# Samples' attention one pair of heads later, the last key pages in two parts, and the output projection's first unit split ahead of the samples' outputs

## The chip, the core and the metric

The kernel runs on one core of one Trainium2 chip. The metric is the device time of one execution in microseconds (us), and lower is better. The engines are named as in the profile: PE is TensorE's matmuls, PEld its weight loads, DVE is VectorE, ACT is ScalarE, POOL is GpSimd, SP is SyncE (here it only issues DMAs, as SPq). PE's clock is granted at one of two levels, 1.2 GHz (0.50 in the profile's column PEclk) and 2.4 GHz (1.00).

## What is computed

One inference step of a two-layer decoder, all in float32, for a prompt of 256 tokens and for 8 samples with one new token each and 256 cached keys in two pages. Layer 0 is gated linear attention and a dense SwiGLU; then a shared key/value projection; layer 1 is stick-breaking attention and a top-2-of-8 mixture of experts. The part that matters here is layer 1's mixer, for both groups of tokens:

```python
def stick_breaking_attention(q, k, v, bias, q_offset):
    ...
        z = jnp.einsum('bqhd,bkhd->bhqk', qb, kb) * (SB_HEAD_DIM ** -0.5) + bias_f
        ...
        log1m = jnp.where(mask, jax.nn.log_sigmoid(-z), 0.0)
        later = lax.cumsum(log1m, axis=3, reverse=True) - log1m
        log_att = jnp.where(mask, log1m + z + later, -jnp.inf)
        outs.append(jnp.einsum('bhqk,bkhd->bqhd', jnp.exp(log_att), vb))

def sb_mixer(h, k_all, v_all, q_offset, w_q, b_sb, w_out):
    ...
    o = stick_breaking_attention(q, k_all, v_all, b_sb, q_offset)
    return o.reshape(B, L, D_MODEL) @ w_out
```

Beside it the conditioning vectors go through the modulation weights (`silu(c) @ ada_w`), of which six weight tiles are multiplied inside this stage.

## The kernel before

**The stage.** Eight pairs of heads of the prompt are worked through by one loop over `g` that every engine runs in its own hand-written order, g = 0 to 8. In step g PE does the sums over later keys of pair g (`later_sums`, L1096 and L1099), the values of pair g - 1 (`values`, L1111), perhaps one modulation tile (`ada`, L763), and the scores of pair g + 2 (`z_products`, L1080 to L1087). ACT turns scores into soft terms (`soft`, L1705 to L1707), takes the exponent (L1720) and rounds pair g - 1 to its high part (L1723). DVE finishes the soft term of pair g + 1 (`softplus`, L2235) and makes the low part of pair g - 1 (L2261).

**The samples' attention** is threaded through the same loop. DVE multiplies each sample's query with its two key pages and reduces by head (page 0: L2213 and L2215, page 1: L2219 and L2221), four pages in `scores_after(1)`, step 0. Then come the bias and an absolute value on DVE (L2267, L2269), an exponent and a logarithm on ACT (L1728, L1729), L2272 on DVE (it posts `l_s`), three small matmuls on PE (L1166 to L1168), L2275 on DVE and L1732 on ACT. From then on PE can multiply the value pages: `values_s(i)` (L1126) for i = 0 to 3, two samples each, in the steps that `OWN_DURING` gives; DVE picks the heads' own parts (`own_values`, L2251) and PE brings them into rows (`own_rows`, L1136). Once the last is there, ACT rounds the samples' rows (L1736), DVE takes the rest (L2280, it posts `os_lo`), and PE starts the output projection `sb_out`.

**The output projection** takes its weights in units: ACT copies a unit's high part (`w_hi`, L1463) and DVE makes its low part (`w_lo`, L1863), and PE needs both for L845 to L847. Its first three units wait for the end of the loop (`first_splits`).

**The weight ring.** Three buffers of 2 MB, `ring0` to `ring2`, are filled by SP strictly in the order of the list `STREAM`; before each load SP waits until the tile that lies in that buffer was used. In this stage the tiles are called here by their kind and number: a22 to a27 (modulation, `ada`), v0 to v3 (value pages), k0 to k3 (key pages), o0 and o1 (`sb_out`), a28 to a31 (the final norm's modulation, `in_final_ada_w`). The order of the loads is

```python
+ [("ada", 22)] + [t for i in range(4) for t in (("ada", 23 + i), ("v_cache", i))] + [("ada", 27)]
+ [("sb_out", i) for i in range(2)] + [("ada", i) for i in range(28, 32)])
```

that is a22, a23, v0, a24, v1, a25, v2, a26, v3, a27, o0, o1, a28. With three buffers in turn, v0 goes where k3 was, a24 where a22 was, v1 where a23 was, a25 where v0 was, and so on. A load of v0 waits until both pages of the last two samples were reduced (`z_s_ready`), one of a25 until `values_s(0)` was done (`opv_done`).

The tables that set in which step PE multiplies them are

```python
PAGES_AFTER = (((1, 4), (1, 5)), ((0, 6), (0, 7), (1, 6), (1, 7)))
ADA_DURING = {1: 22, 2: 23, 3: 24, 4: 25, 6: 26, 7: 27}
OWN_DURING = {2: 0, 3: 1, 5: 2, 6: 3}
```

Of the kernel before, what the change touches and what calls it, by code (L numbers as in the profile page):

```python
# [112 lines left out]
UNIT_AT = {t: 4 * n for n, t in enumerate(SPLIT)}  # L113
# [11 lines left out]
ELSEWHERE = 1000.0  # L125
Q_ROWS = 3
PAGES_DURING = {4: (0, 0), 5: (0, 1), 6: (1, 0), 7: (1, 1), 9: (0, 2), 10: (0, 3), 11: (1, 2), 12: (1, 3), 14: (0, 4), 15: (0, 5)}
PAGES_AFTER = (((1, 4), (1, 5)), ((0, 6), (0, 7), (1, 6), (1, 7)))
ADA_DURING = {1: 22, 2: 23, 3: 24, 4: 25, 6: 26, 7: 27}
OWN_DURING = {2: 0, 3: 1, 5: 2, 6: 3}  # L130
TURNS = [(t, q) for q in range(4) for t in range(TT)]
TURN_AFTER = {5: 0, 6: 1, 7: 2, 9: 3, 10: 4, 11: 5, 13: 6, 14: 7, 15: 8}

# [6 lines left out]
def build(nc, A, O, cap=CAP):  # L140
# [3 lines left out]
    with ctx:  # L144
# [584 lines left out]
        def _(eng):  # L729
# [419 lines left out]
            for g in range(G + 1):  # L1149
                if g < G:  # L1150
                    later_sums(g)
                if g in OWN_DURING and OWN_DURING[g] >= 1:
                    own_rows(OWN_DURING[g] - 1, g - 1)
                if g == 0:
                    eng.wait_ge(S["kv_kept"], 12)
                    eng.wait_ge(S["qs_kept"], 1)
                if g >= 1:
                    values(g - 1)
                if g in ADA_DURING:
                    ada(4 * ADA_DURING[g], 4 * ADA_DURING[g] + 4, ends=g == G - 1)  # L1160
                if g + 2 < G:
                    z_products(g + 2)
                if g == 1:
                    eng.wait_ge(S["l_s"], 1)
                    neg = pb[5][:, 0:P].rearrange("p (b h) -> p b h", b=NB), pb[5][:, P:2 * P].rearrange("p (b h) -> p b h", b=NB)
                    eng.matmul(neg[0], neg_after[:], ls[:, 0, :, :], start=True, stop=False, skip_group_check=True)  # L1166
                    eng.matmul(neg[0], neg_ones[:], ls[:, 1, :, :], start=False, stop=True, skip_group_check=True)
                    eng.matmul(neg[1], neg_after[:], ls[:, 1, :, :], start=True, stop=True, skip_group_check=True).then_inc(S["rcs_done"], 1)  # L1168
                if g in OWN_DURING:
                    values_s(OWN_DURING[g])  # L1170
# [271 lines left out]
        def _(eng):  # L1442
# [41 lines left out]
            def first_splits(kind, first=0):  # L1484
                for m in range(first, AHEAD):
                    split(UNIT_AT[kind, 0] + m, late=True)
# [213 lines left out]
            def soft(g):  # L1700
                eng.wait_ge(S["z_done"], g + 1)
                if g >= 2:
                    eng.wait_ge(S["rc_done"], g - 1)
                lg = l_buf[:, g % 2, :, :]
                link(eng.activation(lg, z_banks(g), ACT.Abs))  # L1705
                link(eng.activation(lg, lg, ACT.Exp, scale=-1.0))
                eng.activation(lg, lg, ACT.Ln, bias=1.0).then_inc(S["soft_ready"], 1)  # L1707
# [7 lines left out]
            for g in range(G + 1):  # L1715
                if g < G:
                    eng.wait_ge(S["rc_done"], g + 1)
                    if g >= 2:
                        eng.wait_ge(S["pv_done"], g - 1)
                    eng.activation(p_buf[:, g % 2, :, :], z_banks(g), ACT.Exp).then_inc(S["p_exp"], 1)  # L1720
                if g >= 1:
                    eng.wait_ge(S["pv_done"], g)
                    eng.copy(hh[:, g - 1, 0:TP], pb[4][:, 0:TP]).then_inc(S["hh_ready"], 1)  # L1723
                if g in ADA_DURING:
                    ada(4 * ADA_DURING[g], 4 * ADA_DURING[g] + 4, ends=g == G - 1)
                if g == 1:
                    eng.wait_ge(S["abs_s"], 1)
                    link(eng.activation(ls, ls, ACT.Exp, scale=-1.0))  # L1728
                    eng.activation(ls, ls, ACT.Ln, bias=1.0).then_inc(S["soft_s"], 1)  # L1729
                if g == 2:  # L1730
                    eng.wait_ge(S["args_s"], 1)
                    eng.activation(zs[:, :, :, 0:SH], zs[:, :, :, 0:SH], ACT.Exp).then_inc(S["exps_s"], 1)  # L1732
                if g + 2 < G:
                    soft(g + 2)
            eng.wait_ge(S["os_done_all"], NB // 2)
            eng.copy(hh[:, :, TP:T], rows_s).then_inc(S["os_hi"], 1)  # L1736
            first_splits("sb_out")
            split_during("sb_out", 2)

            norm(FFN1, splits=False, after=(S["kept_dve"], empt[-1][1]), during=(112, 120))  # L1740
# [104 lines left out]
        def _(eng):  # L1845
# [20 lines left out]
            def first_splits(kind, first=0):  # L1866
                for m in range(first, AHEAD):
                    split(UNIT_AT[kind, 0] + m, late=True)
# [370 lines left out]
            def scores_after(part):  # L2239
                for page, b in PAGES_AFTER[part]:  # L2240
                    (page1_scores if page else page0_scores)(b)
# [12 lines left out]
            for g in range(G + 1):  # L2254
                if g + 1 < G:
                    softplus(g + 1)
                if g == 0:
                    scores_after(1)
                if g >= 1:
                    eng.wait_ge(S["hh_ready"], IN_SB_OUT * KC + g)  # L2260
                    eng.tensor_tensor(hl[:, g - 1, 0:TP], pb[4][:, 0:TP],  # L2261
                                      hh[:, g - 1, 0:TP], ALU.subtract).then_inc(S["hl_ready"], 1)
                if g in ADA_DURING:
                    ada(4 * ADA_DURING[g], 4 * ADA_DURING[g] + 4, ends=g == G - 1)
                if g == 0:
                    eng.wait_ge(S["z_s_ready"], NB)
                    link(eng.tensor_tensor(as_rows(z_of_s), as_rows(z_of_s), sb_bias[:].unsqueeze(1).to_broadcast([P, PAGES * NB, SH]),  # L2267
                                           ALU.add))
                    eng.scalar_tensor_tensor(as_rows(ls), as_rows(z_of_s), -1.0, as_rows(z_of_s), ALU.mult, ALU.max).then_inc(S["abs_s"], 1)  # L2269
                if g == 1:  # L2270
                    eng.wait_ge(S["soft_s"], 1)
                    eng.scalar_tensor_tensor(as_rows(ls), as_rows(z_of_s), 0.0, as_rows(ls), ALU.max, ALU.add).then_inc(S["l_s"], 1)  # L2272
                if g == 2:
                    eng.wait_ge(S["rcs_done"], 1)
                    eng.tensor_tensor(as_rows(z_of_s), as_rows(z_of_s), pb[5][:, 0:256].rearrange("p (r h) -> p r h", h=SH),  # L2275
                                      ALU.add).then_inc(S["args_s"], 1)
                if g in OWN_DURING:
                    own_values(OWN_DURING[g])
            eng.wait_ge(S["os_hi"], 1)
            eng.tensor_tensor(hl[:, :, TP:T], rows_s, hh[:, :, TP:T], ALU.subtract).then_inc(S["os_lo"], 1)  # L2280
            first_splits("sb_out")
            for i in range(8):
                add_block("sb_out", i, GATE[MIX1])

# [240 lines left out]
```

## Time and profile before

| | us |
|---|---|
| median of 3 runs | 1565.06 |
| lowest, highest | 1559.33, 1565.71 |
| the profiled execution | 1560.55 |
| its span, first to last instruction | 1558.7 |
| PE busy in the span | 1499.7 (96%) |
| DVE busy | 440.3 (28%) |
| ACT busy | 325.9 (21%) |

The stage that the change touches runs from about 509 to 586 us of the span. The timeline has one line for each run of like instructions: start, duration, engine, line, what it writes and reads, how many, and in brackets how long the engine sat idle before it and what ended that. A table of stretches has for each stretch its length, each engine's busy time with its number of instructions, PE's granted clock, the mean busy share of the 16 DMA engines and the GB/s that they moved. PE's matmuls overlap, so the distance from one start to the next says more than a duration.

### The profile page before, as it was taken

The numbers are of one execution on the slowest core, as the hardware profiler recorded it, in microseconds if no ns is written. First come the engines' busy times: TensorE is split into PE (matmuls) and PEld (weight loads), VectorE is DVE, ScalarE is ACT, GpSimd is POOL, SyncE is SP. The second block draws the span as 40 slices with busy tenths as digits, with TensorE's granted clock in tenths as the row PEclk, the third lists the DMA queues.
The fourth block names the chain that finished last, engine by engine and source line by source line (L and its number), as shares of the span: only waits on it lengthen the run. The fifth ranks groups of instructions, "written<-read, shape, count | busy, mean of one in ns | idle before, by whom it ended". The sixth has DMA issues, their size and how long they took to land.

```text
span 1558.7 us, 35713 instructions
## 1 busy us (share of the span) xinstructions
PE 1499.7 (96%) x16405; PEld 894.4 (57%) x16405; DVE 440.3 (28%) x697; ACT 325.9 (21%) x505; POOL 60.1 (4%) x111
## 2 busy tenths in 40 slices
PE   6999899999999899899999999999999999999996
PEld 3995688899899557434435435335345344354353
DVE  3653663455477625210010010010020100100312
ACT  3653353444364544200000000000000000000001
POOL 2001100000000000000000000000000000001000
PEclk9999999999999899899999999999999999999996
DMA  9657878884476995999999999999999999999980
GB/s 341 234 200 268 306 267 276 311 295 172 166 264 260 372 396 217 407 365 412 405 403 424 409 405 422 410 409 410 417 411 406 415 416 406 405 425 407 409 372 30
DMA packets 118518, 535.54 MB, mean 344 GB/s; under 512 B 6347, under 2 KB 29001, under 8 KB 88674
## 3 DMA queue, kind: packets, MB, share of 16 engines
q1 hardware_dynamic: 109842, 504.42, 82.3%
q0 software_dynamic: 7584, 25.57, 4.6%
q10 hardware_dynamic: 944, 3.26, 0.6%
q8 instruction: 131, 2.15, 0.6%
q14 instruction: 17, 0.14, 0.0%
HBM read 521.38 MB, written 11.84 MB: 342 GB/s over the span
## 4 chain that ended last, share of the span: by engine, by line
PE 73%; issue 16%; DVE 4%; DMA 3%; ACT 1%; POOL 1%; SPq 0%; POOLq 0%; DVEq 0%; ACTq 0%
PE psum L1256 37%; PE psum L1268 18%; PE psum L845 3%; PE psum L846 3%; PE psum L847 3%; PE psum L763 2%; PE psum L810 1%; PE psum L961 1%; DMA ring<-in_ada_w 1%; DMA xe_rows<-h_rows,row_from 1%; DVE w_lo L1863 1%; PE psum L1269 1%; DMA ring<-in_cache_k 0%; PE psum L929 0%; DMA h<-q_scratch 0%
## 5 line engine op out<-in xcount | busy, mean ns | idle before, releaser
L1256 PE MATMUL psum<-e_ring,xe 128*32 128x512 f32 (+1 forms) x3456 | 336.1, 547 | 0.9 <-DVE xe L2372 0.9
L845 PE MATMUL psum<-hh,w_hi 128*128 128x264 f32 x864 | 250.5, 290 | 9.1 <-DVE hl L1992 2.6
L1256 PE MATMUL psum<-ring,xe 128*32 128x384 f32 (+1 forms) x2688 | 251.9, 531 | 0.0
L846 PE MATMUL psum<-hl,w_hi 128*128 128x264 f32 x864 | 246.6, 285 | 0.0
L847 PE MATMUL psum<-hh,w_lo 128*128 128x264 f32 x864 | 246.4, 285 | 0.0
L1256 PEld LDWEIGHTS psum<-e_ring,xe 128*32 128x32 f32 x3456 | 113.2, 110 | 217.7 <-issue 216.5
L1863 DVE TENSOR_TENSOR w_lo<-ring,w_hi 128x1024 fp32r<-128x1024 f32 (+1 forms) x132 | 157.7, 1206 | 141.2 <-ACT w_hi L1463 141.1
L2415 DVE TENSOR_TENSOR act_e<-silu_e,psum 128x1536 f32<-128x1536 f32 (+1 forms) x16 | 24.9, 1554 | 583.3 <-PE psum L1256 583.3
L1268 PE MATMUL psum<-ring,at 128*32 128x256 f32 x2448 | 180.4, 379 | 0.0
L1269 PE MATMUL psum<-ring,at 128*32 128x256 f32 x816 | 180.0, 379 | 0.0
L1256 PEld LDWEIGHTS psum<-ring,xe 128*32 128x32 f32 x2688 | 87.8, 110 | 159.7 <-issue 159.7
L845 PEld LDWEIGHTS psum<-hh,w_hi 128*128 128x128 f32 x864 | 164.6, 190 | 20.5 <-issue 12.4
L846 PEld LDWEIGHTS psum<-hl,w_hi 128*128 128x128 f32 x864 | 164.8, 191 | 0.0
L847 PEld LDWEIGHTS psum<-hh,w_lo 128*128 128x128 f32 x864 | 163.9, 190 | 0.0
L1463 ACT CAST w_hi<-ring 128x1024 fp32r<-128x1024 f32 (+1 forms) x132 | 135.8, 1034 | 106.3 <-PE psum L847 67.0
L1268 PEld LDWEIGHTS psum<-ring,at 128*32 128x32 f32 x2448 | 100.5, 110 | 71.0 <-issue 3.1
L1268 PE MATMUL psum<-e_ring,at 128*32 128x256 f32 x1584 | 115.6, 379 | 0.0
L1269 PE MATMUL psum<-e_ring,at 128*32 128x256 f32 x528 | 115.5, 379 | 0.0
L1789 ACT ACTIVATE silu_e<-psum 128x1536 f32<-128x1536 f32 (+1 forms) x16 | 20.6, 1290 | 439.4 <-PE psum L1256 439.4
L1268 PEld LDWEIGHTS psum<-e_ring,at 128*32 128x32 f32 x1584 | 65.6, 110 | 44.8
L1269 PEld LDWEIGHTS psum<-ring,at 128*32 128x32 f32 x816 | 89.2, 110 | 0.0
L1770 ACT COPY xe<-psum 128x384 f32<-128x384 f32 x8 | 3.8, 478 | 309.6 <-PE psum L1247 309.6
(401 smaller groups left out, 1235.4 us busy)
## 6 DMA issues: line engine op xcount, KB each, us to landing
e_ring<-in_moe_w_gate_up SPq DMA_DIRECT2D x40, 2048.0 KB, 13.3
ring<-in_moe_w_gate_up SPq DMA_DIRECT2D x24, 2048.0 KB, 15.4
e_ring<-in_moe_w_gate_up SPq DMA_DIRECT2D x32, 1536.0 KB, 13.0
ring<-in_moe_w_gate_up SPq DMA_DIRECT2D x32, 1536.0 KB, 12.4
ring<-in_ada_w SPq DMA_DIRECT2D x20, 2048.0 KB, 11.0
ring<-in_moe_w_down SPq DMA_DIRECT2D x24, 1536.0 KB, 12.6
ring<-in_moe_w_down SPq DMA_DIRECT2D x16, 2048.0 KB, 9.9
e_ring<-in_moe_w_down SPq DMA_DIRECT2D x16, 2048.0 KB
```

What stands on the lines that cost most here:

```text
L763: last = eng.matmul(part_bank(i)[g * STRIP:(g + 1) * STRIP, :], c_pad[:, k, :], cols8(slot("ada", i))[:, at, :], start=half == 0 and i == ...
L810: last = eng.matmul(pb[7][:, 0:T], ones[:], squares[:, k, :], start=k == 0, stop=k == KC - 1)
L845: eng.matmul(to, wh, ah, start=start, stop=False)
L846: eng.matmul(to, wh, al, start=False, stop=False)
L847: return eng.matmul(to, wl, ah, start=False, stop=stop)
L1256: last = eng.matmul(outs[r][s * STRIP:(s + 1) * STRIP, :].rearrange("p (c i) -> p c i", c=4), tokens[:, r * STRIP:(r + 1) * STRIP], pieces ...
L1268: eng.matmul(outs[r][strip, :], tokens[:, strip], w, start=start, stop=stop, skip_group_check=True)
L1269: last = eng.matmul(outs[r][CAP:P, :], tokens[:, r * STRIP:(r + 1) * STRIP], rest, start=start, stop=stop, skip_group_check=True)
L1463: eng.copy(unit(w_hi, kind, m, ks), quarter(slot(kind, i), kind, m % 4, ks)).then_inc(S["hi_ready"], 1)
L1789: eng.activation(silu_e[:, 0:ROUNDS * width].rearrange("p (r c) -> p r c", r=ROUNDS), psum[:, 0:ROUNDS * 512].rearrange("p (r c) -> p r c" ...
L1863: eng.tensor_tensor(unit(w_lo, kind, m, ks), quarter(slot(kind, i), kind, m % 4, ks), unit(w_hi, kind, m, ks), ALU.subtract).then_inc(S["l ...
L2415: eng.tensor_tensor(by_round(act_e), by_round(silu_e), psum[:, 3 * 512:6 * 512].rearrange("p (r c) -> p r c", r=ROUNDS)[:, :, 0:width], AL ...
```

## The change

The samples' chain, from the bias to the exponent, moves one step of g later on all three engines, and `values_s` moves to steps 3, 4, 5 and 6. The page 1 products of the last two samples (4 of the 8 instructions of `scores_after(1)`) move from step 0 to step 1 of DVE. a25 moves from step 4 to step 5. ACT and DVE split `sb_out`'s first unit before they wait for the samples' rows. What SP issues, and its order, stay as they are.

```diff
-PAGES_AFTER = (((1, 4), (1, 5)), ((0, 6), (0, 7), (1, 6), (1, 7)))
-ADA_DURING = {1: 22, 2: 23, 3: 24, 4: 25, 6: 26, 7: 27}
-OWN_DURING = {2: 0, 3: 1, 5: 2, 6: 3}
+PAGES_AFTER = (((1, 4), (1, 5)), ((0, 6), (0, 7)), ((1, 6), (1, 7)))
+ADA_DURING = {1: 22, 2: 23, 3: 24, 5: 25, 6: 26, 7: 27}
+OWN_DURING = {3: 0, 4: 1, 5: 2, 6: 3}
...
-                if g == 1:
+                if g == 2:
                     eng.wait_ge(S["l_s"], 1)
...
-                if g == 1:
+                if g == 2:
                     eng.wait_ge(S["abs_s"], 1)
...
-                if g == 2:
+                if g == 3:
                     eng.wait_ge(S["args_s"], 1)
...
+            split(UNIT_AT["sb_out", 0], late=True)
             eng.wait_ge(S["os_done_all"], NB // 2)
             eng.copy(hh[:, :, TP:T], rows_s).then_inc(S["os_hi"], 1)
-            first_splits("sb_out")
+            first_splits("sb_out", 1)
...
-                if g == 0:
+                if g == 1:
+                    scores_after(2)
                     eng.wait_ge(S["z_s_ready"], NB)
...
-                if g == 1:
+                if g == 2:
                     eng.wait_ge(S["soft_s"], 1)
...
-                if g == 2:
+                if g == 3:
                     eng.wait_ge(S["rcs_done"], 1)
...
+            split(UNIT_AT["sb_out", 0], late=True)
             eng.wait_ge(S["os_hi"], 1)
             eng.tensor_tensor(hl[:, :, TP:T], rows_s, hh[:, :, TP:T], ALU.subtract).then_inc(S["os_lo"], 1)
-            first_splits("sb_out")
+            first_splits("sb_out", 1)
```

**PE, steps 2 and 3.** `ring0` is a23 or v1, `ring1` is v0 and `ring2` is a24 here. Before, from a23 to a24:

```order
L763 MATMUL psum<-ring0,c_pad 32x512 x8
L1080 MATMUL psum<-bias_r,sixty_fourth 128x384 x2
L1083 MATMUL psum<-never,ident_r 128x256 x2
L1087 MATMUL psum<-kvq 128x128 x6
L1126 MATMUL psum<-ring1,work3 32x512 x8
L1096 MATMUL psum<-work3,neg_after 128x384 x2
L1099 MATMUL psum<-work3,neg_ones 128x128 x2
L1136 MATMUL psum<-work3 128x2x2 x4
L1111 MATMUL psum<-work3 64x128 x6
L763 MATMUL psum<-ring2,c_pad 32x512 x8
```

Afterwards, from the three small matmuls on, two rows behind a23:

```order
L1166 MATMUL psum<-work3,neg_after 128x128
L1167 MATMUL psum<-work3,neg_ones 128x128
L1168 MATMUL psum<-work3,neg_after 128x128
L1096 MATMUL psum<-work3,neg_after 128x384 x2
L1099 MATMUL psum<-work3,neg_ones 128x128 x2
L1111 MATMUL psum<-work3 64x128 x6
L763 MATMUL psum<-ring2,c_pad 32x512 x8
L1080 MATMUL psum<-bias_r,sixty_fourth 128x384 x2
L1083 MATMUL psum<-never,ident_r 128x256 x2
L1087 MATMUL psum<-kvq 128x128 x6
L1126 MATMUL psum<-ring1,work3 32x512 x8
```

Before, v0 (`ring1`) was used between a23 and a24; afterwards a24 (`ring2`) is used first and v0 behind it, while they are still loaded in the order v0, a24.

**DVE, the last four pages.** Before, they stand in one row, then the samples' bias:

```order
L2213 TENSOR_TENSOR ring<-ring,h 128x1024
L2215 TENSOR_REDUCE work<-ring 128x16
L2213 TENSOR_TENSOR ring<-ring,h 128x1024
L2215 TENSOR_REDUCE work<-ring 128x16
L2219 TENSOR_TENSOR ring<-ring,h 128x1024
L2221 TENSOR_REDUCE work<-ring 128x16
L2219 TENSOR_TENSOR ring<-ring,h 128x1024
L2221 TENSOR_REDUCE work<-ring 128x16
L2267 TENSOR_TENSOR work<-work,sb_bias 128x16x16
L2269 SCALAR_TENSOR_TENSOR work<-work 128x256
L2235 SCALAR_TENSOR_TENSOR work<-psum,work 128x768
L2261 TENSOR_TENSOR hl<-psum,hh 128x256
```

Afterwards (the lines' numbers are higher by one or two):

```order
L2214 TENSOR_TENSOR ring<-ring,h 128x1024
L2216 TENSOR_REDUCE work<-ring 128x16
L2214 TENSOR_TENSOR ring<-ring,h 128x1024
L2216 TENSOR_REDUCE work<-ring 128x16
L2236 SCALAR_TENSOR_TENSOR work<-psum,work 128x768
L2262 TENSOR_TENSOR hl<-psum,hh 128x256
L2220 TENSOR_TENSOR ring<-ring,h 128x1024
L2222 TENSOR_REDUCE work<-ring 128x16
L2220 TENSOR_TENSOR ring<-ring,h 128x1024
L2222 TENSOR_REDUCE work<-ring 128x16
L2269 TENSOR_TENSOR work<-work,sb_bias 128x16x16
L2271 SCALAR_TENSOR_TENSOR work<-work 128x256
```

The soft term of pair 2 and the low part of pair 0 now stand ahead of the last two pages.

**ACT, the end of the loop**, as a difference:

```order
 L1723 CAST hh<-psum 128x256
-L1736 CAST hh<-psum 128x8x8
-L1463 CAST w_hi<-ring 128x1024 x8
+L1463 CAST w_hi<-ring 128x1024
+L1737 CAST hh<-psum 128x8x8
+L1463 CAST w_hi<-ring 128x1024 x7
```

One of the eight copies of `w_hi` now stands ahead of the rounding of the samples' rows.

## Rows read from the trace of the kernel before

**Rows 1.** Timeline of DVE: the last four pages, pair 2's terms, then L2272.

```profile
525.08 1.22 DVE L2219 TENSOR_TENSOR ring<-ring,h 128x1024 f32<-128x1024 f32 x1
...
528.71 1.22 DVE L2221 TENSOR_REDUCE work<-ring 128x16 f32<-128x1024 f32 x1
...
530.77 0.95 DVE L2235 SCALAR_TENSOR_TENSOR work<-psum,work 128x768 f32<-128x768 f32 x1
531.64 0.41 DVE L2261 TENSOR_TENSOR hl<-psum,hh 128x256 fp32r<-128x256 f32 x1
531.97 0.41 DVE L2272 SCALAR_TENSOR_TENSOR work<-work 128x256 f32<-128x256 f32 x1
```

**Rows 2.** Timeline of PE, steps 1 to 4 of the loop.

```profile
532.44 0.76 PE L1166 MATMUL psum<-work,neg_after 128*128 128x128 f32 x2 [2.51 <-DVE work L2272]
...
533.84 2.49 PE L1096 MATMUL psum<-work,neg_after 128*128 128x384 f32 x4
...
542.85 1.56 PE L1096 MATMUL psum<-work,neg_after 128*128 128x384 f32 x4
...
544.68 0.95 PE L1136 MATMUL psum<-work 128*128 128x4 f32 x8
545.57 0.88 PE L1111 MATMUL psum<-work 128*64 128x128 f32 x12
546.38 1.92 PE L763 MATMUL psum<-ring,c_pad 128*32 128x512 f32 x16
548.23 0.59 PE L1080 MATMUL psum<-bias_r,sixty_fourth 128*128 128x384 f32 x2
...
550.02 1.92 PE L1126 MATMUL psum<-ring,work 128*32 128x512 f32 x16
...
555.00 1.92 PE L763 MATMUL psum<-ring,c_pad 128*32 128x512 f32 x16 [0.31 <-DMA ring<-in_ada_w]
```

**Rows 3.** Stretches: length, busy of PE, PEld, DVE, ACT, POOL; clock, DMA share, GB/s.

```profile
532.50:535.90 3.40, 3.40 (x10) 2.49 (x11) 0.96 (x1) 1.67 (x2) 0.00 (x0) 0.50 0.96 349
536.00:578.00 42.00, 41.59 (x353) 23.33 (x356) 9.77 (x17) 18.36 (x27) 0.00 (x0) 1.00 1.03 400
583.80:590.50 6.70, 4.88 (x22) 4.91 (x23) 4.63 (x4) 3.30 (x4) 0.00 (x0) 0.50 1.05 391
```

**Rows 4.** Timeline of SP's DMA queue: the loads of v0, a24 and a25.

```profile
529.96 2.08 SPq L512 DMA_DIRECT2D ring<-in_cache_v  x4
532.08 0.46 SPq L525 DMA_DIRECT2D ring<-in_ada_w  x1
...
543.05 0.39 SPq L525 DMA_DIRECT2D ring<-in_ada_w  x1
```

**Rows 5.** DMA issues by stretch, KB each, us to landing: a25, o0, then two final ones.

```profile
ring<-in_ada_w SPq DMA_DIRECT2D x1, 2048.0 KB, 11.9
...
ring<-in_sb_w_out SPq DMA_DIRECT2D x1, 2048.0 KB, 9.5
...
ring<-in_final_ada_w SPq DMA_DIRECT2D x2, 2048.0 KB, 8.6
```

**Rows 6.** DMA packets of the stretches 544.0 to 544.5 and 544.5 to 545.0.

```profile
DMA packets 56, 0.20 MB, mean 410 GB/s; under 512 B 7, under 2 KB 7, under 8 KB 55
...
DMA packets 53, 0.20 MB, mean 393 GB/s; under 512 B 5, under 2 KB 5, under 8 KB 53
```

**Rows 7.** Timeline of ACT in step 1, of SP's o0 and o1, of PE and ACT at the end.

```profile
526.50 0.37 ACT L1723 CAST hh<-psum 128x256 fp32r<-128x256 f32 x1
...
571.84 2.08 SPq L539 DMA_DIRECT2D ring<-in_sb_w_out x2
...
576.09 1.06 PE L763 MATMUL psum<-ring,c_pad 128*32 128x512 f32 x8
...
585.62 0.56 PE L845 MATMUL psum<-hh,w_hi 128*128 128x264 f32 x1 [2.55 <-issue]
...
583.21 3.89 ACT L1463 CAST w_hi<-ring 128x1024 fp32r<-128x1024 f32 x4
```

## The prediction

> **What bounds the kernel now.** I read the page first for where PE works, then the timeline of all engines from 500 to 600 us, the only stretch the change touches, then the DMA's packets there. Outside that stretch nothing is reordered, so the question is one number: when PE starts the output projection, 585.62 us of the span now [rows 7]. Everything behind it follows PE and moves with it.
>
> In the stretch two things run side by side at their limit. PE was busy for 41.59 of the 42 us from 536 to 578, at the full clock, and the DMA engines had a share of 1.03 at 400 GB/s in the same time [rows 3]. PE lost time at two places: it waited 2.51 us for `l_s` until 532.44 [rows 2] and then ran at the 0.50 clock until 535.9 [rows 3], and it waited 2.55 us until 585.62 [rows 7], again with 0.50 after it [rows 3]. These are the places that the change aims at. The weight ring is nearly as late as PE: a25 was issued at 543.05 [rows 4], took 11.9 us [rows 5], so it landed at 554.95, and PE waited 0.31 us for it [rows 2].
>
> **Part 1, the pages in two parts.** Now the four pages run on DVE from before 525.08 and end at 528.71 + 1.22 = 529.93, and 0.03 us later SP issues v0 [rows 1, 4]. In the changed order pair 2's soft term comes ahead of the last two pages: 0.87 us (530.77 to 531.64), to 525.95. Then the low part of pair 0, which needs ACT's rounding that ended at 526.50 + 0.37 = 526.87 [rows 7]; it starts at about 526.95 and takes 0.33 (531.64 to 531.97), to 527.3. The last two pages take the same 4.85 us (525.08 to 529.93), to 532.15. So v0 is issued 2.2 us later, and a24 behind it on SP's queue too, at 534.3 instead of 532.08. Both ends of this cost: 0.87 + 0.33 = 1.2 us if DVE does not idle, 2.2 with the idle time; I take 2.2.
>
> **Part 2, the samples' chain one step later.** PE now goes on at 532.44 - 2.51 = 529.93 without `l_s`. Until it wants a24 it does, by distances in rows 2: later sums 1.83 (542.85 to 544.68), values 0.81, a23 1.85, scores 1.79 (548.23 to 550.02), the three small matmuls 0.8 (1.40 at half clock, 532.44 to 533.84, so 0.7 at full), later sums 1.83, values 0.81. That is 9.72 us, to 539.65. `l_s` is ready: the bias and ACT's two passes end near 535, the small matmuls come at 536.2. So the wait of 2.5 us and the half-clock phase, worth 3.4 / 2 = 1.7 us, do go.
>
> **What is late next is a24.** Its landing has no row, but packets show it: modulation tiles in 8 KB packets alone are not "under 8 KB". From 544.0 to 544.5 there was one such packet (56 against 55), from 544.5 to 545.0 none (53 of 53) [rows 6]. So a24 landed about 544.8, 1.6 us before PE used it at 546.38 [rows 2]. The loads behind v0 are 2.2 us later, so now it lands at 547.0. PE stands at it from 539.65, 7.3 us. The gain of part 2 is swallowed whole.
>
> **And the ring closes.** Before, PE took a23, v0, a24 in the order in which they are loaded. Afterwards it takes a24 ahead of v0 (the order of PE shown above), and a25 can't be issued until v0's buffer is free, which is when `values_s(0)` ends. From a24 to there PE does a24 and scores, 3.64 us (546.38 to 550.02), and `values_s(0)`, 1.92: 5.56 us. After a wait this long the clock falls: the two phases at 0.50 after waits of 2.5 us lasted 3.4 and 6.7 us [rows 3], which costs 1.7 to 3.4 us, and I take 2.5. So `values_s(0)` ends at 547.1 + 5.56 + 2.5 = 555.1 (554.3 to 556.0). a25 is issued then, 12 us later than now, while v1 is long issued and landed: the DMA queue runs dry for some 5 us.
>
> From there the loads set the pace again. A 2 MB tile into a queue that was nearly empty took 8.6 us [rows 5], so a25 lands at 563.7. Five tiles lie from a25 to o0 (v2, a26, v3, a27, o0): a25 landed at 554.95 and o0 at 571.84 + 9.5 = 581.34 [rows 5, 7], 26.4 us, 5.3 each. So a27 lands at 584.8 and o0 at 590.1. PE's work from a25's issue up to a27 is less than these 29.7 us (some 27 us by the distances of rows 2), so PE waits for a27.
>
> **Part 3, the first unit split in front.** With today's landings it would pay: o0 landed at 581.34, but ACT started its split at 583.21, and 2.41 us later PE began [rows 7]; about 1.5 us would go. With o0 at 590.1 it doesn't matter where the split stands. ACT copies from 590.1, DVE follows, PE starts 2.41 us later, at 592.5. The samples' rows are no earlier: from a27's first half at 576.09 to the start of the split at 583.21 were 7.1 us [rows 7], so they are ready at 584.8 + 7.1 = 591.9. The split in front of them now holds them back by up to its own wait for o0; with both so near that costs nothing more.
>
> **The sum.** 592.5 - 585.62 = 6.9 us later. The half clock at the start of the projection, 4.9 us of it after 585.62 [rows 3], stays in either case, since PE again waits there more than once: 0 (between -2.5 if it is gone and +1.5 if it already holds during a27). Against the profiled execution's 1560.55 that gives 1567.4. That execution lies 4.5 us under the median of 1565.06, two of three runs lie at 1565 to 1566 and one at 1559.33; the sum is a difference, so on the median it gives 1572.0. I put the forecast a little under that, 1571, as some of the runs will be of the lower kind.
>
> On the pace of the ring the Trainium skill ("DMA: Bandwidth & Descriptors", section Bandwidth) puts the ceiling at 435 GB/s. At that rate a tile of 2.1 MB takes 4.8 us instead of 5.3 and the sum would be 2.4 us less, +4.5. The trace has 400 GB/s over 42 us [rows 3], and the sum goes by that.
>
> **The rivals.**
>
> *PE sets the end (faster).* If the loads kept up, PE would gain 2.5 + 1.7 us in the loop, and 1.5 us from the early split: -5.7, with the half clock gone too up to -8. So 1557 to 1560 on the median. It decides on a24: it would have to land before 539.65 after being issued at 534.3, and the shortest time here for such a tile is 8.6 us into a nearly empty queue [rows 5]. Against it is that v0 stands ahead of it. 0.07. The Trainium skill ("Perfetto Trace Analysis", section Identifying Performance Opportunities) says that a kernel gains by the most-contended engine. By it PE, busy 41.59 of 42 us, would be the one to relieve, and the time would be this rival's.
>
> *Only the shift, without the closed ring.* If v0's tile is used soon after a24 because the clock does not fall and the queue still has v1 in it, the DMA's gap is 2 to 3 us, and o0 lands 4 to 5 us late, of which 1.9 (581.34 to 583.21) is slack and 0.5 to 1 is given back by the early split: +0 to +3, 1565 to 1568. 0.13.
>
> *The wait cascades (slower).* Each long wait puts PE at 0.50 for up to 6.7 us. If `values_s(0)` is done wholly at half clock (5.56 us more, not 2.5) or if a27's wait also drops the clock, so that a27, the last values and rows run at half speed (7.1 us with some 4 of work), 2 to 5 us more are lost in a row: +9 to +12, 1574 to 1577. It decides from a low phase of more than about 5 us after a24's wait. 0.20.
>
> *As summed.* +4.5 to +9, 0.60; two thirds of it under 7.8 us.
>
> **Chances and range.** What a measurement of this kernel tells from no change is about 0.5%, 7.8 us. Within it: 0.40 of the likeliest, 0.13 of the shift, 0.04 of the faster one, 0.57. Slower by more: 0.20 + 0.20 = 0.40. Faster by more: 0.03. The range goes from 1562 (a small gain or the shift in a run of the lower kind) to 1577 (the end of the cascade).
>
> **What would show it.** In the new trace: no wait of PE for `l_s` and PE at a24 near 540; a wait of 5 to 8 us there, ended by the DMA of `in_ada_w`; half clock behind it; v0's issue at about 532.2 and a25's at about 555 instead of 543; a stretch of 4 to 6 us with little DMA near 550 to 556; a wait for a27; the projection at about 592. I am wrong at the root if a24 is used before 544, if a25's issue is earlier than 550, or if the DMA never runs dry. I am wrong in size if the pace of the later tiles isn't 5.3 us or the low clock lasts much longer.

## The result and the profile after

The changed kernel is slower, by a little and beyond doubt of its sign: 1565.51 us (median of 20 runs, 1561.49 to 1568.15) against 1560.91 us for the kernel before (20 runs, 1557.33 to 1565.71). The ratio is 1.0026, with a 95% interval of 1.0017 to 1.0035, so 2.7 to 5.5 us. The median of before over 20 runs lies 4.15 us under that of the three runs known ahead (1565.06).

The profiled execution of the changed kernel has a span of 1564.3 us, against 1558.7. PE is busy for as long as before. What grew is the part of the chain that ended last which was a DMA: 5% of the span, where it was 3%. That share alone proves nothing: in e2 below, which is faster than before, it is 6%. From the page of the changed kernel, busy times and the chain:

```profile
PE 1500.1 (96%) x16405; PEld 891.9 (57%) x16405; DVE 440.2 (28%) x697; ACT 325.9 (21%) x505; POOL 60.3 (4%) x111
...
PE 72%; issue 16%; DMA 5%; DVE 4%; ACT 1%; POOL 1%; SPq 0%; POOLq 0%; DVEq 0%; ACTq 0%
```

**Where to measure from.** Two executions differ already before the stage. Its first scores start at 508.99 us in the profile of before and at 510.97 in that of the changed kernel, and in those of the experiments between 505.73 and 511.48, though no kernel differs in anything that runs ahead of them. So distances are taken from this row (L1080) on, which is called the entry. The projection starts at 585.62 before [rows 7], 76.63 us after the entry. Of the timeline of PE in the changed kernel:

```profile
510.97 0.59 PE L1080 MATMUL psum<-bias_r,sixty_fourth 128*128 128x384 f32 x2
...
530.62 0.88 PE L1111 MATMUL psum<-work 128*64 128x128 f32 x12
534.07 3.46 PE L763 MATMUL psum<-ring,c_pad 128*32 128x512 f32 x16 [2.58 <-DMA ring<-in_ada_w]
...
539.09 0.49 PE L1166 MATMUL psum<-work,neg_after 128*128 128x128 f32 x2
...
546.77 3.02 PE L763 MATMUL psum<-ring,c_pad 128*32 128x512 f32 x16 [4.21 <-DMA ring<-in_ada_w]
...
551.88 1.92 PE L1126 MATMUL psum<-ring,work 128*32 128x512 f32 x16
...
578.88 1.92 PE L1126 MATMUL psum<-ring,work 128*32 128x512 f32 x16 [2.40 <-DMA ring<-in_cache_v]
...
584.34 1.07 PE L763 MATMUL psum<-ring,c_pad 128*32 128x512 f32 x8 [0.80 <-DMA ring<-in_ada_w]
...
592.14 0.59 PE L845 MATMUL psum<-hh,w_hi 128*128 128x264 f32 x1 [0.86 <-DVE hl L2283]
```

The wait for `l_s` of [rows 2] is gone (539.09 has no bracket). In its place PE waits 2.58 us for a23 (534.07), 4.21 for a24 (546.77), 2.40 for v3 (578.88) and 0.80 for a27 (584.34), each time for a load, and 0.49 for v2 (568.32). The projection starts at 592.14, 81.17 us after the entry, 4.54 later than before. The first sums of squares behind the projection (L810) start at 616.84, where they start at 611.14 in before's profile. From the entry these are 105.87 and 102.15 us, 3.72 later. It is less than 4.54 because the half clock behind the start of the projection is shorter: it was granted until 590.5 before, 4.9 us behind 585.62 [rows 3], and until about 595.5 now, 3.4 us behind 592.14. The two medians differ by 4.60 us, and the ratio makes it 4.1.

SP's queue shows why. Its rows in the changed kernel, v0, a24, v1, a25, v2:

```profile
533.14 2.08 SPq L512 DMA_DIRECT2D ring<-in_cache_v  x4
535.26 0.43 SPq L525 DMA_DIRECT2D ring<-in_ada_w  x1
537.68 1.92 SPq L512 DMA_DIRECT2D ring<-in_cache_v  x4
553.95 0.39 SPq L525 DMA_DIRECT2D ring<-in_ada_w  x1
554.43 1.94 SPq L512 DMA_DIRECT2D ring<-in_cache_v  x4
```

a25 was issued at 543.05 before [rows 4]; now SP sits before it until 553.95, 0.15 us after `values_s(0)` (551.88 + 1.92). Nothing is issued for 14 us (from 539.6 on), and the queue empties. The stretches of the changed kernel, in the columns of [rows 3]:

```profile
543.00:546.50 3.50, 0.00 (x0) 0.00 (x0) 0.75 (x2) 0.42 (x1) 0.00 (x0) 1.00 0.98 413
547.30:550.60 3.30, 3.30 (x19) 1.15 (x12) 0.00 (x0) 0.00 (x0) 0.00 (x0) 0.52 0.97 394
550.70:555.00 4.30, 4.30 (x35) 2.20 (x34) 1.05 (x2) 2.50 (x3) 0.00 (x0) 0.98 0.05 16
555.50:588.00 32.50, 27.97 (x237) 15.27 (x236) 6.41 (x13) 11.29 (x17) 0.00 (x0) 1.00 1.02 393
592.00:595.50 3.50, 3.36 (x16) 3.36 (x17) 3.08 (x4) 2.37 (x3) 0.00 (x0) 0.54 1.07 430
```

The third is the one to see: for 4.3 us PE computes and the DMA engines stand (share 0.05, 16 GB/s). Before and behind it they run at 0.98 and 1.02. PE, on the other hand, has 4.5 us of slack in the 32.5 behind it, 3.7 of them in waits for loads (0.49, 2.40 and 0.80). So the loads pace this part of the stage, and an idle stretch of theirs comes out as time.

The end of the loop looks unlike the forecast. ACT and DVE in the changed kernel, from the last pair's rounding on:

```profile
589.28 0.37 ACT L1723 CAST hh<-psum 128x256 fp32r<-128x256 f32 x1 [1.56 <-PE psum L1111]
589.65 1.05 ACT L1463 CAST w_hi<-ring 128x1024 fp32r<-128x1024 f32 x1
591.32 0.21 ACT L1737 CAST hh<-psum 128x64 fp32r<-128x64 f32 x1 [0.62 <-PE psum L1136]
```

```profile
590.73 1.23 DVE L1864 TENSOR_TENSOR w_lo<-ring,w_hi 128x1024 fp32r<-128x1024 f32 x1 [0.62 <-ACT w_hi L1463]
591.87 0.22 DVE L2283 TENSOR_TENSOR hl<-psum,hh 128x64 fp32r<-128x64 f32 x1
```

o0 was issued at 576.62 and landed 13.0 us later, at 589.62. ACT, free from 589.65, begins the early split without a wait and is through when the samples' rows are there, and PE starts 0.27 us after 591.87, where DVE begins their low part.

### The profile page after: what moved, and what is told of

It is laid out like the page before. It is cut to its first block, busy times and chain, and to the rows that moved or that the text cites. A ratio compares the mean times of both kernels' runs of the same rounds, so it can differ in the third digit from the quotient of the medians.

```text
span 1564.3 us, 35713 instructions
## 1 busy us (share of the span) xinstructions
PE 1500.1 (96%) x16405; PEld 891.9 (57%) x16405; DVE 440.2 (28%) x697; ACT 325.9 (21%) x505; POOL 60.3 (4%) x111
## 4 chain that ended last, share of the span: by engine, by line
PE 72%; issue 16%; DMA 5%; DVE 4%; ACT 1%; POOL 1%; SPq 0%; POOLq 0%; DVEq 0%; ACTq 0%
PE psum L1256 37%; PE psum L1268 18%; PE psum L845 3%; PE psum L846 3%; PE psum L847 3%; PE psum L763 2%; PE psum L810 1%; DMA ring<-in_sb_w_out 1%; DMA ring<-in_cache_v 1%; PE psum L961 1%; DMA ring<-in_ada_w 1%; DVE w_lo L1864 1%; DMA xe_rows<-h_rows,row_from 1%; PE psum L1269 1%; DMA ring<-in_cache_k 1%
## 5 line engine op out<-in xcount | busy, mean ns | idle before, releaser
L845 PE MATMUL psum<-hh,w_hi 128*128 128x264 f32 x864 | 250.2, 290 | 8.2 <-DVE w_lo L1864 3.3
L845 PEld LDWEIGHTS psum<-hh,w_hi 128*128 128x128 f32 x864 | 164.2, 190 | 19.6 <-issue 9.7
L763 PE MATMUL psum<-ring,c_pad 128*32 128x512 f32 x512 | 66.7, 635 | 7.7 <-DMA ring<-in_ada_w 7.6
```

The lines of the kernel that those rows point to most:

```text
L763: last = eng.matmul(part_bank(i)[g * STRIP:(g + 1) * STRIP, :], c_pad[:, k, :], cols8(slot("ada", i))[:, at, :], start=half == 0 and i == ...
L845: eng.matmul(to, wh, ah, start=start, stop=False)
```

## The experiments

All are measured against the kernel before, which shared their chips. The table is made from their timelines and times; "a25" is SP's issue of it and "projection" PE's first L845, both from the entry, as is "L810", the first sums of squares.

| kernel | entry | a25 | projection | L810 | median, runs | ratio to before, 95% |
|---|---|---|---|---|---|---|
| before | 508.99 | 34.06 | 76.63 | 102.15 | 1560.91, 20 | |
| changed | 510.97 | 42.98 | 81.17 | 105.87 | 1565.51, 20 | 1.0026 (1.0017 to 1.0035) |
| e1, a24 in step 4 | 507.90 | 33.88 | 75.89 | 101.81 | 1559.94, 12 | 0.9999 (0.9986 to 1.0012) |
| e2, loads in order of use | 506.88 | 33.75 | 75.21 | 101.02 | 1558.55, 12 | 0.9986 (0.9974 to 0.9997) |
| e3, pages not in parts | 511.48 | 43.13 | 81.13 | 107.18 | 1564.68, 12 | 1.0017 (1.0003 to 1.0030) |
| e4, early split alone | 510.34 | 34.84 | 75.48 | 100.36 | 1558.63, 12 | 0.9985 (0.9973 to 0.9997) |
| e5b, the swap alone | 510.01 | 41.14 | 81.08 | 105.97 | 1564.77, 12 | 1.0021 (1.0007 to 1.0036) |
| e6b, no early split | 510.20 | 41.90 | 81.58 | 107.00 | 1569.13, 6 | 1.0049 (1.0030 to 1.0067) |
| e7b, e2 and e3 together | 505.73 | 33.56 | 73.80 | 98.66 | 1557.53, 12 | 0.9975 (0.9963 to 0.9987) |

e1 to e4 stand against 35 runs of before with a median of 1560.58, e5b to e7b against 23 with 1561.33. Three more, e5, e6 and e7, have no time; e5b, e6b and e7b are the same kernels. The columns from "entry" to "L810" come from one execution each.

The theory is that the cost comes from the ring: PE uses a24 ahead of v0, which are loaded the other way round, so SP can't issue a25. The rivals are that the later chain or the pages in two parts cost the time (the loads of v0 and a24 are late), or that it is the half clock behind the waits.

**e1: the order of use set right by PE.** In the changed kernel, a24 goes behind `values_s(0)`:

```diff
-ADA_DURING = {1: 22, 2: 23, 3: 24, 5: 25, 6: 26, 7: 27}
+ADA_DURING = {1: 22, 2: 23, 4: 24, 5: 25, 6: 26, 7: 27}
```

> The changed kernel with one number changed: a24 is multiplied in step 4 of the loop instead of step 3, so PE takes a23, v0, a24, v1 again in the order in which they are loaded. Theory (the closed ring): the wait of PE for a24 (4.21 us at 546.77 in the changed kernel) goes, a25 is issued right behind v0's use, near 546 instead of 554, the DMA never runs dry, and of the loss only v0's later issue (1.2 us) is left, which the early split covers: the projection starts 76 to 77.5 us after the stage's first scores (76.6 before, 81.1 changed), the time is within 1.5 us of the kernel before. Rival (the later issue of v0, or the pace of the loads, is what costs): the projection stays at 79.5 us or more, the time at +3 us or more.

Timeline of PE in e1, a23, v0, a24 and v1, and the start of the projection:

```profile
531.03 1.92 PE L763 MATMUL psum<-ring,c_pad 128*32 128x512 f32 x16 [1.06 <-DMA ring<-in_ada_w]
...
539.75 1.92 PE L1126 MATMUL psum<-ring,work 128*32 128x512 f32 x16
...
545.13 1.92 PE L763 MATMUL psum<-ring,c_pad 128*32 128x512 f32 x16
...
549.90 1.92 PE L1126 MATMUL psum<-ring,work 128*32 128x512 f32 x16 [1.23 <-DMA ring<-in_cache_v]
...
583.79 0.59 PE L845 MATMUL psum<-hh,w_hi 128*128 128x264 f32 x1 [0.83 <-DVE hl L2283]
```

Its stretches from 541 to 560:

```profile
541.00:545.00 4.00, 4.00 (x36) 2.81 (x28) 1.59 (x2) 2.17 (x3) 0.00 (x0) 1.00 1.00 412
545.00:560.00 15.00, 12.61 (x113) 6.81 (x109) 2.41 (x4) 5.13 (x8) 0.00 (x0) 1.00 1.02 409
```

v0 is used first, a25 issued at 541.78, the DMA never runs dry there, and with that the loss against before is gone: 75.89 us to the projection instead of 81.17, and a ratio of 0.9999. The pages in two parts, the chain one step later and the later steps of the value pages are still in it, so none of them is the main cost. The early split is in it too; what the rest costs is read against e4 below.

**e2: the order of use set right by SP.** PE stays as in the changed kernel, and the list of loads follows its order of use:

```diff
-+ [("ada", 22)] + [t for i in range(4) for t in (("ada", 23 + i), ("v_cache", i))] + [("ada", 27)]
++ [("ada", i) for i in (22, 23, 24)] + [("v_cache", 0), ("v_cache", 1), ("ada", 25), ("v_cache", 2), ("ada", 26), ("v_cache", 3), ("ada", 27)]
```

> The changed kernel with only the order of the loads changed: a24 is loaded ahead of v0, as PE now takes them. Theory (the closed ring): a24 lands near 542 instead of 546.8, v0 is used near 547, a25 can be issued once a24 is used, near 545, the DMA doesn't run dry; projection 76 to 78 us after the first scores, time within 1.5 us of before. Rival (the later issue of v0 costs, whatever the order): +3 us or more, as the changed kernel.

Timeline of PE in e2, a23, a24, v0, and the start of the projection:

```profile
530.39 3.21 PE L763 MATMUL psum<-ring,c_pad 128*32 128x512 f32 x16 [2.99 <-DMA ring<-in_ada_w]
...
538.57 1.93 PE L763 MATMUL psum<-ring,c_pad 128*32 128x512 f32 x16
...
542.05 1.92 PE L1126 MATMUL psum<-ring,work 128*32 128x512 f32 x16
...
582.09 0.59 PE L845 MATMUL psum<-hh,w_hi 128*128 128x264 f32 x1 [0.63 <-DVE hl L2283]
```

PE meets both tiles without a wait, and the stage takes 75.21 us, 1.42 less than before and 0.27 less than e4, which has the early split alone. The same cause is lifted from the other side with the same result. The wait for a23 stays, 2.99 us: PE no longer stands for `l_s` ahead of it, and comes to it before it has landed.

**e3: the pages back in one part.** In the changed kernel:

```diff
-PAGES_AFTER = (((1, 4), (1, 5)), ((0, 6), (0, 7)), ((1, 6), (1, 7)))
+PAGES_AFTER = (((1, 4), (1, 5)), ((0, 6), (0, 7), (1, 6), (1, 7)), ())
```

> The changed kernel with the last four key pages back in step 0, so v0 is issued as early as before; the samples' chain and the values one step later and the early split stay. Theory (the closed ring): PE still stands at a24 for 2 to 4 us and a25 is issued only after v0's use behind it, so the DMA still runs dry; +2.5 to +3.5 us against before, some 1.2 us less than the changed kernel. Rival (v0's later issue is the cause): the loss goes, within 1 us of before.

Timeline of PE in e3, the later sums of step 1, a24, and the start of the projection:

```profile
533.35 2.47 PE L1096 MATMUL psum<-work,neg_after 128*128 128x384 f32 x4 [4.08 <-DVE work L2236]
...
547.39 3.60 PE L763 MATMUL psum<-ring,c_pad 128*32 128x512 f32 x16 [2.73 <-DMA ring<-in_ada_w]
...
592.61 0.59 PE L845 MATMUL psum<-hh,w_hi 128*128 128x264 f32 x1 [0.87 <-DVE hl L2283]
```

SP issues v0 at 532.46, 20.98 us after the entry as in before (529.96 - 508.99 = 20.97) [rows 4], where it is 22.17 in the changed kernel. So part 1 costs 1.2 us at that issue. It makes no difference behind it: PE uses a24 35.91 us after the entry instead of 35.80, a25 is issued at 43.13 instead of 42.98, the projection starts at 81.13 instead of 81.17. a24 took 12.8 us to land from its issue here and 11.5 in the changed kernel. PE's new wait of 4.08 us for pair 2's soft term, which now stands behind the pages on DVE, and the half clock behind it, also come out as nothing, since PE stands for a24 anyway. So v0 and a24 issued 1.2 us earlier didn't bring a24's landing forward; why not isn't shown. What did come earlier is the end of the loads ahead of the stop. Around 38 to 40 us after the entry the DMA share is 0.20 in e3 (549.5 to 551.5) and 0.81 in the changed kernel (549.0 to 551.0): the queue ran dry earlier, and the gain was waited away there. The times agree: 1.0017 (1.0003 to 1.0030) can't be told from 1.0026.

**e4: the early split alone.** In the kernel before, on ACT and on DVE:

```diff
+            split(UNIT_AT["sb_out", 0], late=True)
             eng.wait_ge(S["os_done_all"], NB // 2)
...
-            first_splits("sb_out")
+            first_splits("sb_out", 1)
```

> The kernel before with part 3 alone: the first unit of the output projection is split ahead of the samples' rows. Theory: o0 landed at 581.34 and ACT began at 583.21, so the projection starts 1.2 to 1.6 us earlier, and up to 2.4 us more go if the clock then stays up: -1 to -4 us against before. Rival (it does nothing because another wait stands there): 0.

Timeline of PE in e4, the wait for `l_s` and the start of the projection:

```profile
533.79 0.80 PE L1166 MATMUL psum<-work,neg_after 128*128 128x128 f32 x2 [3.99 <-DVE work L2273]
...
585.82 0.39 PE L845 MATMUL psum<-hh,w_hi 128*128 128x264 f32 x1 [0.85 <-DVE hl L2282]
```

PE waits 0.85 us before the projection and no longer 2.55 [rows 7]. To the projection it is 1.15 us less than before, and to the L810 behind it 1.79. The ratio of 0.9985 (0.9973 to 0.9997) is the gain of part 3 by itself, some 2 us.

**e5b: the swap alone.** In the kernel before, the samples' chain, the pages and the splits stay, and only the two tables of steps change:

```diff
-ADA_DURING = {1: 22, 2: 23, 3: 24, 4: 25, 6: 26, 7: 27}
-OWN_DURING = {2: 0, 3: 1, 5: 2, 6: 3}
+ADA_DURING = {1: 22, 2: 23, 3: 24, 5: 25, 6: 26, 7: 27}
+OWN_DURING = {3: 0, 4: 1, 5: 2, 6: 3}
```

> The kernel before with two tables changed and nothing else: the value pages are multiplied in steps 3, 4, 5 and 6 and a25 in step 5, so a24 is used ahead of v0. The samples' chain, the key pages and the splits stay where they were. Theory (the closed ring): v0 is issued as early as before, but a25 only once v0 was used behind a24, near 41.5 us after the stage's first scores instead of 34.1; the DMA runs dry for 3 to 5 us before it; the projection starts at 80 to 82 us (76.6 before); +3 to +5 us. Rival (the moved chain or pages cost, not the order of use): within 1 us of before.

Timeline of PE in e5b, a24, v0, and the start of the projection, and then its stretch with little DMA:

```profile
545.61 1.92 PE L763 MATMUL psum<-ring,c_pad 128*32 128x512 f32 x16 [0.94 <-DMA ring<-in_ada_w]
...
549.09 1.92 PE L1126 MATMUL psum<-ring,work 128*32 128x512 f32 x16
...
591.09 0.56 PE L845 MATMUL psum<-hh,w_hi 128*128 128x264 f32 x1 [2.55 <-issue]
```

```profile
547.00:552.50 5.50, 5.50 (x46) 2.82 (x39) 1.34 (x2) 2.50 (x3) 0.00 (x0) 1.00 0.36 121
```

This edit alone makes the projection 4.45 us late (81.08 against 76.63), with a ratio of 1.0021. The long wait for a24 is not needed for it: it was 0.94 us here, and the clock behind it stayed at 1.00. So the half clock is not needed for the loss, and as its main cause it falls. What stayed is a25's issue, at 551.15, 41.14 us after the entry, and a DMA share of 0.36 over 5.5 us while PE is busy throughout.

**e6b: the early split undone.** In the changed kernel, on ACT and on DVE:

```diff
-            split(UNIT_AT["sb_out", 0], late=True)
             eng.wait_ge(S["os_done_all"], NB // 2)
...
-            first_splits("sb_out", 1)
+            first_splits("sb_out")
```

> The changed kernel with the first unit of the projection split behind the samples' rows again. In the changed kernel the early copy ran from 589.65, once the last pair was rounded, so o0 had landed by then and the copy was not held by it, other than the prediction had it. Theory: without the early split the projection starts 1.4 to 1.7 us later (82.6 to 82.9 us after the first scores instead of 81.2), time +1.5 us against the changed kernel, +5 to +6.5 against before. Rival (as predicted: with o0 late the place of the split doesn't matter): 81.2 us, the changed kernel's time, +4.

Timeline of PE in e6b, a24 and the start of the projection:

```profile
546.56 1.93 PE L763 MATMUL psum<-ring,c_pad 128*32 128x512 f32 x16 [2.89 <-DMA ring<-in_ada_w]
...
591.78 0.56 PE L845 MATMUL psum<-hh,w_hi 128*128 128x264 f32 x1 [2.56 <-issue]
```

From the issue of a25 to the projection are 39.68 us (591.78 - 552.10) here and 38.19 in the changed kernel (592.14 - 553.95), and to the L810 65.10 and 62.89. So the early split gives 1.5 us in the changed kernel and 2.2 with the clock phase behind it. The medians give 3.6 us (1569.13 against 1565.51), from only 6 runs of this kernel, of which the profiled one was the shortest. Which of the two sizes is right is open; that it is not nothing is not.

**e7b: loads in order of use, and the pages in one part.** e2 with e3's edit:

> The kernel with the loads in PE's order (a24 ahead of v0), and the last four key pages back in step 0, so a24 and v0 are issued 1.2 us earlier. If the loads set the end of this stage, the projection starts about 1 us earlier than with the pages in two parts (74 to 75 us after the first scores, 75.2 there), although PE then waits some 4 us for pair 2's soft term. If PE sets it, the projection starts later, at 76.5 us or more.

Timeline of PE in e7b, the later sums of step 1, a23, a24, v0, v3 and the start of the projection, and then its stretch from 532 to 580:

```profile
527.60 1.56 PE L1096 MATMUL psum<-work,neg_after 128*128 128x384 f32 x4 [0.94 <-DVE work L2236]
...
530.33 1.92 PE L763 MATMUL psum<-ring,c_pad 128*32 128x512 f32 x16
...
537.23 1.92 PE L763 MATMUL psum<-ring,c_pad 128*32 128x512 f32 x16
...
540.71 1.92 PE L1126 MATMUL psum<-ring,work 128*32 128x512 f32 x16
...
566.28 1.92 PE L1126 MATMUL psum<-ring,work 128*32 128x512 f32 x16 [1.64 <-DMA ring<-in_cache_v]
...
579.53 0.39 PE L845 MATMUL psum<-hh,w_hi 128*128 128x264 f32 x1 [0.86 <-DVE hl L2283]
```

```profile
532.00:580.00 48.00, 42.91 (x362) 24.91 (x358) 12.15 (x24) 20.59 (x31) 0.00 (x0) 1.00 1.03 400
```

With the ring open the 1.2 us of the pages seem to count: 73.80 us to the projection, 1.41 less than e2. The same edit gave nothing in e3. This rests on one profile of each; the intervals of the two ratios, 0.9963 to 0.9987 and 0.9974 to 0.9997, overlap. This is the fastest kernel of the study, 0.9975 (0.9963 to 0.9987), 2.83 us less than before to the projection. Its DMA share is 1.03 over 48 us at full clock, and PE has 5.1 us of slack in them, 2.4 of it in waits for loads (v3 1.64, a27 0.79), so the loads still set the pace at the end of the loop. Its profiled execution was the shortest of its 12 runs; the median says 3.8 us less than before.

**Put together**, to the projection and in the profiles: the swap alone costs 4.45 us (e5b against before). From e5b to the changed kernel a25's issue moves back by another 1.84 (42.98 against 41.14), and from there to the projection it is 1.75 less (38.19 against 39.94), of which e6b puts 1.5 to the early split. That 4.45 + 1.84 - 1.75 makes 4.54 follows from how the terms are formed and confirms nothing. The 1.84 are for the most part the clock: a24 is used 35.80 us after the entry and 35.60 in e5b, but from there to the end of `values_s(0)` it takes 7.03 us (546.77 to 553.80) and 5.40 in e5b (545.61 to 551.01), where no half clock stands behind a24. In e6b, which is the changed kernel up to the end of the loop, the clock stayed up behind a24 as well, and a25 was issued at 41.90.

**The moved chain and the pages are not free.** e6b differs from e5b by them alone, and e1 from e4 by them and the steps of the tables. The projection is 0.50 and 0.41 us later, L810 1.03 and 1.45, and the medians are 4.4 us (95% interval 1.5 to 6.7, resampled from the single runs) and 1.3 us (-0.5 to 3.0) longer. So e1 comes out like before because the early split covers a loss of its own. In the profiles the swap is by far the largest cost; by the times it is 3.4 us (e5b) to 4.2 us (the changed kernel against e1), and the moved chain with the pages 1.3 to 4.4. One source of the rest can be seen. v0 is issued 1.2 us later, when a23 has nearly landed and little else is in the queue. From 22 to 24 us after the entry, in the changed kernel and then in before:

```profile
533.00:535.00 2.00, 0.93 (x8) 0.27 (x12) 1.93 (x5) 0.83 (x2) 0.00 (x0) 0.70 0.34 86
```

```profile
531.00:533.00 2.00, 0.56 (x3) 0.56 (x4) 1.38 (x3) 1.94 (x4) 0.00 (x0) 0.88 0.86 266
```

The DMA share is 0.34 instead of 0.86 for these 2 us, and in e1 it is 0.40 (530.0 to 532.0). How much of the 1.3 to 4.4 us it makes is open.

## Why the prediction was right and where it was wrong

The forecast was 1571.0 us, within a range of 1562 to 1577, and no change that can be told as the likeliest class. The time came out at 1565.51, inside the range and slower by 0.26%; with 20 runs of each the interval clears 1, so the change can be told. The step that failed is the one in "Chances and range" that took 0.5%, 7.8 us, for what can't be told from no change, and so counted all of +0 to +3 and two thirds of +4.5 to +9 as none, 0.57 in all. No row stood behind the 7.8. It is of the size of the spread of single runs (8.4 us among the 20 of before), while the interval of the difference came out at 1.4 us to either side. Of the forecast's distance of 5.49 us, 4.15 come from the base (1565.06 from three runs, 1560.91 from twenty) and the rest from the sum: it put 5.94 us on the base where 4.60 were measured. The sum before it was shaded down, 6.9 us for the projection, stands against 4.54. The 2.4 us between them are a24's landing ("now it lands at 547.0", 38.0 us after the entry, where 35.80 were measured: -2.2), the half clock behind its wait (-0.9) and the loads from a25 to a27 (+0.7). The first is the term that was most off.

**What bounds the kernel: right, but half said.** The prediction called the ring "nearly as late as PE". e1, e2 and e7b show that it counts as much: in e2 PE's wait for `l_s` is gone and the one in front of the projection is down from 2.55 to 0.63, and the stage became only 1.42 us shorter, of which some 1.2 is the early split of e4. By the Trainium skill ("Perfetto Trace Analysis", section Identifying Performance Opportunities) the most-contended engine is the one to relieve. The prediction took PE, with 41.59 of 42 us busy [rows 3], for that engine. The runs don't bear out that choice in this stage: the DMA engines at 1.03 were the other resource at its limit, and what kept their queue filled (e2 against the changed kernel, e7b against e4) gained.

**Part 1, v0's issue 2.2 us later: mis-sized.** It was 1.20 (22.17 - 20.97). The value taken assumed that DVE idles until ACT's rounding. In the changed kernel's profile DVE went from pair 2's soft term into the low part with no idle time, since ACT had rounded by then, and the other end of the range held, in e1 and e6b too (22.17). The consequence drawn was wrong too: a24's landing did not move with its issue. The prediction's own reading, 544.8, is 35.8 us after the entry of before. With the issue 1.2 us later it is 35.80 in the changed kernel, and with the issue as in before 35.91 in e3 and 35.60 in e5b (e6b, with the later issue, has 36.36). By e3 the term is worth nothing while the ring is closed; by e7b against e2 it is worth 1.41 us, one profile of each, once it is open.

**Part 2, the wait and the half clock go, and a24 is next: right in kind.** The three small matmuls stand at 539.09 with no wait. One wait was missed: a23, 2.58 us, and 3.5 us at 0.54 behind it. By the prediction's distances PE comes to a23 at 529.93 + 1.83 + 0.81 = 532.57, 23.6 us after the entry, and a23 landed at 23.10 (534.07 - 510.97), so with them there is no wait. PE came at 20.5 (531.49), 3.1 us earlier. Part of before's time ahead of `l_s` was half clock and not work: behind a wait of 2.07 us PE ran at 0.50 for 6.7 us there, and at 1.00 in the changed kernel, though the instructions are the same. In before:

```profile
518.80:525.50 6.70, 6.62 (x24) 4.77 (x24) 6.63 (x7) 2.50 (x3) 1.25 (x3) 0.50 1.00 369
```

So the 3.1 us were luck of the clock, and the wait for a23 with the slow phase behind it took them and more. PE then came to a24 at 542.56 (546.77 - 4.21), 31.59 us after the entry where 30.66 were forecast, 0.9 later. a24 landed 11.5 us after its issue where the prediction had 12.7 (544.8 - 532.08), and its issue was 1.0 less late: 2.2 us earlier than forecast. So the wait was 7.3 - 0.9 - 2.2 = 4.2, and the 2.2 are the landing that part 1 had wrong.

**The ring closes: right.** a25 was forecast for 555.1 and issued at 553.95. From the entry that is 8.92 us later than before (42.98 - 34.06) where 12.05 were forecast; on the profile's own clock the two look closer, as the changed kernel's stage began 2.0 us later. The dry stretch of "some 5 us" at 550 to 556 was 4.3 us at 550.7 to 555.0. e1, e2 and e5b show it as the cause from three sides. Mis-sized was the half clock behind a24's wait: 3.3 us at 0.52, costing about 1.6, and not 2.5.

**The pace of the loads: right.** a25 to a27 was put at 29.7 us and took 30.4 (553.95 to 584.34): 9.2 for a25, where 8.6 were taken (that figure was the median of two loads), and then 5.3 a tile as forecast. The DMA ran at 393 GB/s from 555.5 on. The Trainium skill's ceiling of 435 GB/s ("DMA: Bandwidth & Descriptors", section Bandwidth) was reached in none of the long stretches shown: 393 in the changed kernel, 409 in e1, 400 in e7b; the highest of the shown is 430 over 3.5 us (592.0 to 595.5), and only stretches of 2 us come to it or just over it (438 in e1, 549.9 to 551.9). The estimate by that figure, +4.5, agrees with the measured 4.54 only because of the mis-sized terms above.

**Part 3, "it doesn't matter where the split stands": wrong.** The step said that o0 lands at 590.1 and the samples' rows come at 591.9. They were 589.62 and 591.32, so the 1.7 us of ACT's time between them held the split's first copy. The prediction's own numbers had the same 1.8 us: with the split behind the rows PE would have started 2.41 us after 591.9, at 594.3, and not at 592.5. The sum had used the second and so was not harmed; the sentence was wrong. e6b prices that at 1.5 us and more, e4 at 1.2 to 1.8.

**The rivals.** "PE sets the end" fell with a24's wait. "Only the shift, without the closed ring" (+0 to +3) is too small and wrong in mechanism: the ring did close, for 4.3 us and not 2 to 3. The cascade did not come: the half clock ended at 550.6, and PE's waits for v3 and a27 left the clock at 1.00 until 588. "As summed" was +4.5 to +9, and the measured 4.54, or 4.60 by the medians, lies at its lower edge. That it lies inside by 0.04 to 0.1 us is luck.

## What to carry to other kernels

In a ring filled in a fixed order, write the order of use beside the order of loading whenever an edit moves work: two tiles used the other way round cost one buffer's lead, here 4.5 us of 77, though nothing was added. An engine that is busy 99% of a stage is not yet the one that paces it; if the DMA engines are full as well, ask what stops their queue, for time saved on the engine comes back as waits for the next tile. And look at every tile that is met without a wait today: the wait that the edit removes may have been the reason.

## What the runs showed of the hardware

- A wait of 4.21 us on PE was followed by 3.3 us at the 0.52 clock, one of 2.58 by 3.5 at 0.54, one of 2.73 in e3 by a24's matmuls in 3.60 us instead of 1.92. But a wait of 2.89 (a24 in e6b, 1.93) left the clock at full, and so did those of 2.40 (v3) and 0.80 in the changed kernel. Before, two waits of 2.5 us were followed by 3.4 and 6.7 us [rows 3]. The same instructions behind the same wait of 2.07 or 2.08 us, ahead of pair 2's scores, ran for 6.7 us at 0.50 in before and at 1.00 in the changed kernel. The length of the wait does not give that of the slow phase.
- The same code ahead of the stage ended between 505.73 and 511.48 us in nine profiled executions. That is more than the whole effect, and shows why single profiles are compared by distances inside the stage.
- A 2 MB tile took 9.2 us to land into an empty queue (a25, 553.95) and 11.5 to 13.8 us into a running one (a24 and a27), so the empty queue saved a tile 2.3 to 4.6 us of its own time, while the stage lost what was not moved in the 4.3 us.
